# Two projection chunks, one rope copy and the Exp table load change places in the latent-attention loop

## The reference

```python
q_c, kv_c, k_r, z = split(h @ w_in)                     # 256, 128, 64 and 2048 columns
q_c, kv_c = rms_norm_2(q_c), rms_norm_2(kv_c)
q = einsum('bsr,rhd->bshd', q_c, w_uq)                  # 16 heads, 128 nope + 64 rope
q_rope, k_rope = apply_rope(q[..., 128:]), apply_rope(k_r)
q_lat = einsum('bshd,rhd->bshr', q[..., :128], w_uk)
for i in range(4):                                      # blocks of 128 queries
    s = (q_lat[i] @ kv_c.T + q_rope[i] @ k_rope.T) * ATTN_SCALE
    p = softmax(where(key_chunk <= q_chunk, s, -inf))   # chunks of 64
    o_lat[i] = p @ kv_c
o = einsum('bshr,rhd->bshd', o_lat, w_uv)
y = (o * silu(z)) @ w_out
```

## Time and profile before

| | us |
|---|---|
| median of 3 executions | 1973.71 (1973.09 to 1975.76) |
| profiled execution: its time | 1973.71 |
| profiled execution: its span, first to last instruction | 1972.0 |
| TensorE busy | 1928.4 (98% of the span) |
| VectorE, ScalarE, GpSimd busy | 1051.9, 828.3, 793.2 (53%, 42%, 40%) |
| MLA pairs, from the first projection of pair 0 to the last of pair 7's head work | 1612 to 1868 |

### The profile page before, as it was taken

The page is one execution under the profiler, slowest core; times in us unless marked ns, Lnnn a source line. Parts: engine busy times, 40 slices in busy tenths (PEclk is TensorE's granted clock), DMA queues, the critical chain, the costliest instruction groups (busy, mean ns, idle before and its releaser), DMA issues.

```text
span 1972.0 us, 29532 instructions
## 1 busy us (share of the span) xinstructions
PE 1928.4 (98%) x9826; PEld 1624.1 (82%) x9826; DVE 1051.9 (53%) x2323; ACT 828.3 (42%) x1527; POOL 793.2 (40%) x392
## 2 busy tenths in 40 slices
PE   7999999999999999999999999999999999999997
PEld 5898888888878899888888888888788888888886
DVE  5564655321274777546653445666614565666645
ACT  4564322222353777543222323422223356666622
POOL 3633544444354211145444443444544332424441
PEclk9999999999999999999999999999999999999999
DMA  7532555322234112125453332333232221212221
GB/s 239 179 107 96 192 171 180 106 96 96 96 108 141 39 48 79 38 96 202 161 185 107 101 96 86 97 98 105 94 102 97 65 86 54 78 55 80 65 85 43
DMA packets 70020, 209.52 MB, mean 106 GB/s; under 512 B 9739, under 2 KB 15115, under 8 KB 69948
## 3 DMA queue, kind: packets, MB, share of 16 engines
q1 hardware_dynamic: 57724, 174.72, 27.3%
q10 hardware_dynamic: 12224, 33.85, 5.3%
HBM read 196.90 MB, written 8.49 MB: 104 GB/s over the span
## 4 chain that ended last, share of the span: by engine, by line
PE 87%; DVE 5%; issue 2%; ACT 1%; POOL 1%; DVEq 0%; ACTq 0%; POOLq 0%
PE bank L1025 22%; PE bank L1027 22%; PE bank L1026 22%; PE bank L1393 3%; PE bank L1571 2%; PE bank L1590 2%; PE bank L1342 2%; PE bank L1373 1%; PE bank L1445 1%; PE bank L1243 1%; PE bank L1582 1%; PE bank L1450 1%; PE bank L1389 1%; PE bank L1231 1%; POOL wsp L471 1%
## 5 line engine op out<-in xcount | busy, mean ns | idle before, releaser
L471 POOL TENSOR_TENSOR wsp<-raw,wsp 128x1024 fp32r<-128x1024 f32 (+2 forms) x291 | 706.2, 2432 | 933.4 <-ACT wsp L581 930.0
L1025 PE MATMUL bank<-xs,wsp 128*128 128x512 f32 x1304 | 514.7, 395 | 4.7 <-DVE mid L2199 1.7
L581 ACT ACTIVATE wsp<-raw 128x1024 fp32r<-128x1024 f32 (+2 forms) x294 | 302.7, 1037 | 508.7 <-PE bank L1027 465.6
L1027 PE MATMUL bank<-xs,wsp 128*128 128x512 f32 x1304 | 508.9, 390 | 0.0
L1026 PE MATMUL bank<-xs,wsp 128*128 128x512 f32 x1304 | 508.6, 390 | 0.0
L1025 PEld LDWEIGHTS bank<-xs,wsp 128*128 128x128 f32 x1304 | 245.4, 188 | 57.5 <-issue 7.7
L1027 PEld LDWEIGHTS bank<-xs,wsp 128*128 128x128 f32 x1304 | 245.2, 188 | 51.6
L1026 PEld LDWEIGHTS bank<-xs,wsp 128*128 128x128 f32 x1304 | 245.6, 188 | 50.0 <-issue 1.0
L1025 PE MATMUL bank<-gsp,wsp 128*128 128x512 f32 x512 | 200.4, 391 | 1.6 <-issue 1.2
L1027 PE MATMUL bank<-gsp,wsp 128*128 128x512 f32 x512 | 199.6, 390 | 0.0
L1026 PE MATMUL bank<-gsp,wsp 128*128 128x512 f32 x512 | 199.4, 389 | 0.0
(11 more groups left out here) (321 smaller groups left out, 2761.6 us busy)
## 6 DMA issues: line engine op xcount, KB each, us to landing
raw<-weights SPq DMA_DIRECT2D x294, 512.0 KB, 3.5
gen<-ada ACTq DMA_DIRECT2D x48, 512.0 KB, 3.5
tmp<-mid SPq DMA_DIRECT2D x64, 128.0 KB, 2.9
bias_b<-bias_row ACTq DMA_DIRECT2D x1, 4096.0 KB, 37.5
mid<-bias_b SPq DMA_DIRECT2D x8, 512.0 KB, 4.0
hT<-xT SPq DMA_DIRECT2D x2, 1024.0 KB, 9.5
bias_a<-bias_row ACTq DMA_DIRECT2D x1, 2048.0 KB, 17.6
mid<-bias_a SPq DMA_DIRECT2D x8, 256.0 KB, 2.8
```

The source lines that it names most:

```text
L471: pool.tensor_tensor(wsp[:, slot, 1, 0:w], raw[:, slot, 0:w], wsp[:, slot, 0, 0:w].bitcast(F32), ALU.subtract).then_inc(w_ready, 1)
L581: act.activation(wsp[:, u % RING, 0, 0:w], raw[:, u % RING, 0:w], ACT.Copy).then_inc(hi_done, 1)
L1025: pe.matmul(dst, w[0], x[0], start=first, stop=False)
L1027: return pe.matmul(dst, w[1], x[0], start=False, stop=last)
```

## The change

Three edits, all in the MLA pairs.

1. ScalarE: the one-element Exp moves from the head of a pair to the end of the pair before, behind the residual tile; `rope_hi(1)` of the next pair comes directly behind it, instead of behind exp(0). For pair 0 `rope_hi(1)` stands ahead of the loop, and there is no one-element Exp. `split_hi(u0 + 4)` moves from behind exp(1) to behind exp(0).
2. TensorE, `latent_queries`: one wait for both heads' low parts stands ahead of the first matmul, where before each head had its own.
3. TensorE, order of a pair: S0 and S1 come behind all eight chunks of `project(u0)` instead of behind six. Behind S1 three chunks of `project(u0 + 1)` follow, instead of the last two of u0 and one of u0 + 1. The two chunks that stood between V0 and T2 are thereby gone from there.

```diff
             def pair_of_heads(r, hp, last):        # ScalarE
 
                 u0 = O_H + 2 + RING * r
-                act.activation(credit[:, 10:11], eps[:, 0:1], ACT.Exp)
                 for m in range(10):
                     if m >= 2:
                         o_turn(m - 2, r, hp)
                     if m < 8:
                         o_exp_of(m, r, hp)
                     if m == 0:
-                        rope_hi(1, r, hp)
-                    if m == 1:
                         split_hi(u0 + 4, hp)
...
                                bias=modg[:, 1, bass.ds(j + 24, 1)]).then_inc(alpha_done, 1)
+                if not last:
+                    act.activation(credit[:, 10:11], eps[:, 0:1], ACT.Exp)
+                    rope_hi(1, r + 1, hp)
...
             rope_hi(0, 0, 0)
+            rope_hi(1, 0, 0)
             split_hi(O_H + 5)
...
             def latent_queries(r, hp, u):          # TensorE
+                pe.wait_ge(n_ready, hp * 2 + (2 * r + 2))
                 for e in range(2):
-                    pe.wait_ge(n_ready, hp * 2 + (2 * r + e + 1))
...
                 z = [bank[n] for n in GATE_BANKS[r]]
-                project(u0, z[0][:, :], hp, part=range(6))
+                project(u0, z[0][:, :], hp)
                 o_scores(0, r, hp)
                 o_scores(1, r, hp)
-                project(u0, z[0][:, :], hp, part=range(6, DC))
-                project(u0 + 1, z[1][:, :], hp, part=range(1))
-                parts = {4: range(1, 3), 5: range(3, 5), 9: range(5, DC)}
+
+                project(u0 + 1, z[1][:, :], hp, part=range(3))
                 for m in range(2, 11):
-                    if m in parts:
-                        project(u0 + 1, z[1][:, :], hp, part=parts[m])
+                    if m in (5, 9):
+                        project(u0 + 1, z[1][:, :], hp, part=range(3, 5) if m == 5 else range(5, DC))
                     if m < 10:
                         o_transpose(m - 2, r, hp)
```

## The result

The changed kernel takes 1985.3 us (median of 6 runs, 1981.8 to 1988.7) against 1974.0 us (6 runs, 1972.1 to 1975.8) for the kernel before: slower, as predicted, but by 11.3 us where 6.9 were forecast, and 1985.3 lies outside the range of 1977.8 to 1983.2 us. The record holds five further executions of the changed kernel, the profiled one among them. The median of all eleven is 1984.2 us, 10.2 above the kernel before and outside the range too, and the ratio of 1.0052 (95% interval 1.0039 to 1.0065) says about the same. The profiled execution took 1986.4 us around a span of 1984.7 us.

What follows compares the result with a forecast made beforehand. TensorE was taken to bound the kernel (87% of the chain, busy 31.82 of pair 1's 31.90 us). Losses of 2.44 + 3.20 + 1.00 + 0.24 = 6.88 us on 1973.7 gave 1980.6 us, range 1977.8 to 1983.2.

Steps and rivals of the forecast that it cites:

- TensorE's order: Pairs 1, 3, 5, 6: T2 waits 0.73 us for its probabilities and starts 0.61 later; four pairs, 2.44 us.
- The ordinary pair: Any of pairs 1, 3, 5 and 6, without an extra table load: 0.61 us slower each.
- The second load: Pairs 2 and 4: another 1.28 us table load ahead of exp(0) makes T2 1.60 later; 3.20 us in all.
- Rival A: Pairs 2 and 4: the extra table load is free or quicker; sum 4.9, 1978.6 us; chance 0.13.
- Pair 0: First pair: copies wait for rotate(1), then split and table load precede exp(0); T2 1.00 us later.
- Pair 7: Last pair: copies ahead of exp(0) put T2 at 1848.61 instead of 1848.37, 0.24 us later.
- Rival B: At T2: no wait comes, and waits at S0 and T1 go; 1.7 us gained, 1972.0 us; chance 0.03.
- Rival C: Delay spreads at T3, or three loads cost 1.38 more each: 1.6 to 4.1 us added, 1982 to 1985; chance 0.11.
- Rival D: ScalarE's order: S4's copies, never late, come sooner and exp(0) 0.2 us later; already in the forecast, no own time.
- the sum: All pairs: 2.44 + 3.20 + 1.00 + 0.24 = 6.88 us, added to the profiled execution's 1973.7.

Runs made afterwards that it cites:

- Experiment 4: Changed kernel plus a one-element Exp ahead of the loop, so that no table load stands at the loop's head: 1980.6 us, ratio 1.0028.
- experiment 5: Changed kernel with TensorE's chunks put back as before, ScalarE's new order and the common wait kept: 1991.7 us, ratio 1.0088.
- experiments 3 to 7: Besides Experiment 4 and experiment 5: kernel before with TensorE's new order, 1979.8 us; changed kernel with one chunk given back, 1982.5; kernel before with ScalarE's splits later, 1987.2.
- experiment 10: Kernel before with the residual tile's update behind exp(5) and a third of the next pair's queries between V6 and V7: 1969.7 us, ratio 0.9967.
- experiment 9: Kernel before, unchanged, timed once more on another chip: 1975.0 us, ratio 1.0002.

## Why the prediction was wrong in its time and right in its steps

- **TensorE's order.** S0 at 5.45, T0 8.63, T1 9.77, T2 12.31, T3 14.93 were forecast; 5.44, 8.62, 9.73, 12.29, 14.97 came. The wait in front of T2 was forecast at 0.73 us and is 0.63. Right. The ordinary pair lost 0.63 to 0.68 us instead of 0.61: behind T2 there is a further 0.05.
- **The second load.** T2 at 13.30 forecast, 13.29 measured; pair 2 lost 1.65 us, 1.60 forecast. Experiment 4 shows the load's share alone, 0.97 us a pair. Rival A is out. The Trainium skill (ScalarE: Activation LUTs, What ACT_TABLE_LOAD costs) gives about 1283 ns for the load, which agrees with the 1.28 us here, also where the table is the one already loaded. Its drain of about 1380 ns doesn't appear, though this load is a switch, from Silu's set to that of Exp: 1687.89 plus 1.28 is 1689.17, and the next ScalarE instruction starts at 1689.18; in front of the load ScalarE stood 0.02 us.
- **Pair 0** lost 0.43 us in itself and 0.55 by its later start; 1.00 was forecast as one sum. I had written that the common wait hides behind the chain of that pair, and it does: the wait starts the pair 0.55 later, and the chain behind rotate(1) sets its end, 1.0 later. **Pair 7** lost 0.29 instead of 0.24.
- **Rival B** (nothing late at T2) is out by the wait itself. **Rival C**, the spreading, came only as these 0.05 us a pair: no wait stands at T3, and no load costs more than its 1.28 us. The 1982 to 1985 us that it gives is where the measurement lies, by luck and not by its mechanism. **Rival D** has experiment 5 as its measure: ScalarE's order helps only what was never late, and costs 12.4 us where TensorE's doesn't cover it.
- **The step that failed is the sum.** It added the terms in the pairs to the time of one execution and took all code that the change doesn't touch as fixed; "any difference ahead of 1610 us would be one that I don't explain" is how the prediction put it, and no part of the range was set aside for it. Its upper end, 1983.2, came from a part of rival C. The runs show in its place that the code ahead of 1610 us doesn't take a fixed time: against the first profile of before, VectorE's instructions just ahead of the pairs come 5.5, 1.2 and 4.7 us later in the three profiles of the changed kernel, and 0.1 us earlier and 0.5 us later in the other two of before. This is made of a clock that falls near 80 us (2.9, 0.6 and 4.2 us) and of VectorE's additions beside GpSimd (1.8 us near 190 in all three and in the last one of before, in the first profile of the changed kernel 2.1 more near 550); 1.5 us of it is made up again by 887 us. An identical kernel came out 1.0016 of itself.
- **What the range lacked.** The range for one measurement had to carry that: the mechanism's 5.9 to 8.0 us and some 3 to 4 us on top. The three measurements of the changed kernel, 1.0052, 1.0032 and 1.0037, are 10.3, 6.3 and 7.3 us by their ratio; the intervals of the second and the third hold the 7.2 us of the pairs, that of the first (7.7 to 12.8 us) doesn't, and the first is the one that is high. Between the medians of all executions lie 7.2 us. On that measure the 6.9 holds, and it isn't luck, since its steps in the pairs came one by one.
- **What stays open:** why the clock fell near 80 us in the three profiles of the changed kernel and in those of experiments 3 to 7, but not in the three of before or in that of experiment 10. If the program decides it, a part of what the profiles lost there (0.6 to 4.2 us) belongs to the change; no experiment rules that out. The 0.8 us between the 8 at a like mean clock and the 7.2 of the pairs isn't traced either.

## What to carry to other kernels

Work placed between a producer's input and its consumer is cover: before moving it ahead of the input, add up the chain from the input (here maximum, exponential, reciprocal, normalising: 2.36 us) and what is left to do beside it. A table load stood at the loop's head here where the two ways into the loop came with different tables, and one dummy activation ahead of the loop removed it. And a forecast for one measurement needs two widths: that of the mechanism, and that of the unchanged rest, which a second run of the same kernel gives before anything is changed.

## What the runs showed of the hardware

- Loading an activation table that is already the active one costs the full 1.28 us (the loads at L947 in pairs 2 and 4, at 1690.58 and 1756.69 us; that of pair 0 does change the table, since a square root came before it).
- VectorE's addition of 128x512 float32 takes 0.69 us alone and up to 2.96 us while GpSimd subtracts 128x1024 float32; the subtractions took 2.6 us each in the stretch near 190 us of experiment 9 (5.18 for two).
- The mean granted clock of whole executions of one and the same kernel lies between 0.994 and 0.998, and its time between 1971.6 and 1979.3 us.
